# Router logits with stationary router weights, and the counts and context sums in another order

## The reference

```python
p_group = softmax(t @ wg + bg)                     # 4 groups
p_top_g, g_idx = top_k(p_group, 1)
e_logits = einsum('td,gde->tge', t, we) + be        # 4 x 8 experts
e_logits = take_along_axis(e_logits, g_idx[:, :, None], axis=1)[:, 0]
p_top_e, e_idx = top_k(softmax(e_logits), 2)
w_sel = p_top_g * p_top_e / sum(p_top_e)
# combine: w_sel at the two chosen experts of the chosen group, else 0
hid = silu(t @ w_gate[e]) * (t @ w_up[e]) * combine[:, e]     # 32 experts, 512 wide
out = sum over e of hid @ w_down[e]
```

## Time and profile before

| | |
|---|---|
| median of three runs | 1970.4 us (1968.82 to 1971.67) |
| profiled execution | 1971.46 us, its span 1969.6 us |
| busy in the span: TensorE, weight loads, VectorE, ScalarE, GpSimd | 1868.5, 1366.6, 818.2, 586.1, 387.5 us |
| mean granted TensorE clock | 0.978 |
| DMA | 429.84 MB, mean 218 GB/s |
| router: first transpose to first expert's rows | 405.78 to 430.09 us |
| expert stage, end of its last load wait | about 867 us |

### The profile page before, as it was taken

One profiled execution on the slowest core, in us unless ns is written; L12 is line 12 of the kernel. 1 busy time (PEld: TensorE's weight loads), 2 busy tenths in 40 slices (PEclk: granted clock), 3 DMA queues, 4 the chain that ended last, 5 costly groups with the idle time before them and its releaser, 6 DMA issues.

```text
span 1969.6 us, 26164 instructions
## 1 busy us (share of the span) xinstructions
PE 1868.5 (95%) x11248; PEld 1366.6 (69%) x11248; DVE 818.2 (42%) x1342; ACT 586.1 (30%) x892; POOL 387.5 (20%) x205
## 2 busy tenths in 40 slices
PE   5999999999999999999999899999999899889998
PEld 2777796964444343447887657888888688679998
DVE  1615255731111111116343744566655625574333
ACT  2513103331111111113113535223333411544554
POOL 2000000120000000004003132333443210425665
PEclk8999999989999999999999899999999899999999
DMA  9479917669999999992224004454445222414451
GB/s 357 153 256 344 341 44 278 215 270 429 426 427 428 427 427 427 427 394 82 86 86 161 3 33 171 150 181 162 149 150 182 92 91 89 171 47 168 174 196 38
DMA packets 111425, 429.84 MB, mean 218 GB/s; under 512 B 5706, under 2 KB 8821, under 8 KB 98512
## 3 DMA queue, kind: packets, MB, share of 16 engines
q1 hardware_dynamic: 109056, 416.56, 54.5%
q0 software_dynamic: 2256, 11.62, 1.6%
HBM read 427.11 MB, written 1.05 MB: 217 GB/s over the span
## 4 chain that ended last, share of the span: by engine, by line
PE 65%; DMA 17%; DVE 5%; PEld 5%; issue 3%; ACT 3%; POOL 2%; PEldq 0%; SPq 0%; POOLq 0%; DVEq 0%; ACTq 0%
PE bank L556 64%; DMA ring<-in_moe_w_down 7%; PEld bank L556 4%; DMA H<-in_moe_w_down 4%; DMA arena<-in_moe_w_down 4%; DMA ring<-in_ada_w 2%; PE bank L571 1%; PEldq L535 0%; POOL arena L1889 0%; POOL arena L1888 0%; DVE H L1976 0%; DMA ring<-in_w_in 0%; DVE H_low L1983 0%; POOL arena L1893 0%; POOL arena L1891 0%
## 5 line engine op out<-in xcount | busy, mean ns | idle before, releaser
L556 PE MATMUL bank<-arena_r 128*128 128x256 f32 (+1 forms) x2176 | 591.7, 339 | 12.1 <-ACT arena_r L1380 6.1
L556 PE MATMUL bank<-arena_r,ring_low 128*128 128x512 f32 (+2 forms) x1920 | 596.4, 342 | 1.8 <-DVE H_low L1983 1.0
L556 PEld LDWEIGHTS bank<-arena_r 128*128 128x128 f32 x2176 | 384.9, 190 | 63.2 <-issue 18.2
L556 PE MATMUL bank<-arena 128*128 128x64 bf16 (+8 forms) x2908 | 366.1, 319 | 42.7 <-DMA arena<-in_hy_filt_w 11.7
L556 PEld LDWEIGHTS bank<-arena_r,ring_low 128*128 128x128 f32 (+1 forms) x1920 | 352.5, 188 | 47.7 <-issue 2.7
L556 PEld LDWEIGHTS bank<-arena 128*128 128x128 bf16 (+4 forms) x2908 | 206.2, 132 | 203.8 <-issue 168.6
L556 PE MATMUL bank<-H_low,arena_r 128*128 128x512 f32 (+1 forms) x672 | 217.3, 340 | 0.0
L556 PE MATMUL bank<-ring,arena 128*64 128x512 f32 x768 | 172.0, 603 | 8.4 <-DMA ring<-in_moe_w_down 7.9
L2556 DVE SCALAR_TENSOR_TENSOR X<-bank,mod,X 128x256 f32<-128x256 f32 x216 | 94.2, 478 | 196.6 <-PE bank L556 196.6
L1915 POOL TENSOR_TENSOR ring_low<-ring,arena_r 128x2048 fp32r<-128x2048 f32 x31 | 142.3, 4614 | 131.1 <-DVE ring_low L2568 69.1
L1394 ACT ACTIVATE arena<-bank 128x512 f32<-128x512 f32 (+2 forms) x106 | 51.2, 496 | 368.5 <-PE bank L556 368.5
(11 more groups left out here) (304 smaller groups left out, 1845.4 us busy)
## 6 DMA issues: line engine op xcount, KB each, us to landing
ring<-in_w_mlp SPq DMA_DIRECT2D x32, 2048.0 KB, 7.8
ring<-in_w_in SPq DMA_DIRECT2D x26, 2048.0 KB, 9.1
ring<-in_ada_w SPq DMA_DIRECT2D x24, 2048.0 KB, 11.6
ring<-in_moe_w_up SPq DMA_DIRECT2D x17, 2048.0 KB, 23.2
ring<-in_moe_w_gate SPq DMA_DIRECT2D x17, 2048.0 KB, 27.8
arena<-in_moe_w_up SPq DMA_DIRECT2D x15, 2048.0 KB, 22.4
ring<-in_moe_w_down SPq DMA_DIRECT2D x14, 2048.0 KB, 23.3
arena<-in_moe_w_down SPq DMA_DIRECT2D x13, 2048.0 KB, 24.3
```

What stands on the lines that cost most here:

```text
L556: ins = nc.tensor.matmul(o, l, r, start=start, stop=stop, skip_group_check=True)
```

## The change

The logits are computed first: `WR[:, k]` (36 columns) is stationary and the 256 tokens move, one product for each block of `H` as it is normed, into 36 partitions of bank 4. ACT copies them to `LGT`, and two products with the identity turn them back to 2 x 36 columns for VectorE. The transposes of the first token block stand between, those of the second behind. VectorE does two of its four subtractions ahead of the router's logic and two behind it; ACT's exponentials stand between its two middle parts. Only one of the count steps stays ahead of the one-hot columns, the rest goes behind the pair's weights. The first four context sums move from behind the zero products to behind the ranks, the other four behind the first two gathers, and the context's root on ACT behind two copies. Chunk 7 waits for "tokens_passed" 6.

```diff
@@ SP, expert()
                 elif c == MRING - 1:
-                    sp.wait_ge(S("logits"), 1)
+                    sp.wait_ge(S("tokens_passed"), 6)
@@ tiles
+        LGT = A(5000, L)
@@ TensorE
+            def tokens(tb):
+
+                for k in range(KT):
+                    tr(ps[2 * tb + k // 4][:, (k % 4) * P:(k % 4 + 1) * P], H[:, k, tb * P:(tb + 1) * P], "tokens_passed" if k % 4 == 3 else None)
+
+            pe.wait_ge(S("tables_in"), 64)
+            for k in range(KT):
+                pe.wait_ge(S("normed"), 16 + k + 1)
+                mm(ps[4][0:NR, 0:L], WR[:, k, :], H[:, k, 0:L], k == 0, k == KT - 1, "logits" if k == KT - 1 else None)
+            tokens(0)
+            pe.wait_ge(S("rt_exp"), 1)
             for tb in range(TB):
-                for k in range(KT):
-                    if tb == 0:
-                        pe.wait_ge(S("normed"), 16 + k + 1)
-                    tr(ps[2 * tb + k // 4][:, (k % 4) * P:(k % 4 + 1) * P], H[:, k, tb * P:(tb + 1) * P], "tokens_passed" if k % 4 == 3 else None)
-            pe.wait_ge(S("tables_in"), 64)
-            for tb in range(TB):
-                for k in range(KT):
-                    mm(ps[4][:, tb * NR:(tb + 1) * NR], H[:, k, tb * P:(tb + 1) * P], WR[:, k, :], k == 0, k == KT - 1,
-                       "logits" if (tb, k) == (1, 7) else None)
+                mm(ps[4][:, L + tb * NR:L + (tb + 1) * NR], LGT[0:NR, tb * P:(tb + 1) * P], ident[0:NR, 0:NR], inc="logits" if tb else None)
+            tokens(1)
 
             pe.wait_ge(S("selected"), 1)
             pe.wait_ge(S("h_rest"), 4)
             for b in range(4):
                 mm(ps[b], SW[:, 0, :], SW[:, 0:4, :], True, False)
-            for k in range(KT // 2):
-                stat(2, k, L, CSQ)
...
-            for k in range(KT // 2, KT):
+            for k in range(KT // 2):
                 stat(2, k, L, CSQ)
...
             for u in range(2):
                 gather(u, 4 + u, "gathered")
+            for k in range(KT // 2, KT):
+                stat(2, k, L, CSQ)
@@ ScalarE
+            act.wait_ge(S("logits"), 1)
+            A_(LGT[0:NR, :], ps[4][0:NR, 0:L], ACT.Copy).then_inc(S("rt_exp"), 1)
             for b in range(4):
                 act.wait_ge(S("tokens_passed"), 2 + b + 1)
                 A_(by_blocks(HB[:, 0, b // 2, :], b % 2), ps[b][:, :].rearrange("t (p k) -> t k p", k=KT), ACT.Copy).then_inc(S("h_natural"), 1)
...
+            middle_part(0)
+            router_exp(0)
+            router_exp(1)
+            middle_part(1)
             act.wait_ge(S("b2_in"), 16)
             for k in range(KT):
                 square(k, L, CSQ, X[:, :, L:2 * L]).then_inc(S("squares"), 1)
...
+            gathered_out(0)
+            gathered_out(1)
             act.wait_ge(S("sum_ready"), 3)
             link(A_(RS[:, L:2 * L], ps[6][:, 0:L], ACT.Ln, bias=vec("eps")))
             A_(RS[:, L:2 * L], RS[:, L:2 * L], ACT.Exp, scale=-0.5).then_inc(S("rms_ready"), 1)
-            gathered_out(0)
-            gathered_out(1)
@@ VectorE
+            rest_of(0)
+            rest_of(1)
+            dve.wait_ge(S("logits"), 2)
+            link(V.tensor_tensor(LG, ps[4][:, L:L + 2 * NR].rearrange("p (a b) -> p a b", a=2),
                                  bc(vec("rbias", 0, NR).unsqueeze(1), [P, TB, NR]), ALU.add))
...
             V.tensor_tensor(ex, m2, m1, ALU.subtract).then_inc(S("rt_arg"), 1)
-            dve.wait_ge(S("rt_exp"), 2)
+            rest_of(2)
+            rest_of(3)
+            dve.wait_ge(S("rt_exp"), 3)
...
             dve.wait_ge(S("ranks"), 1)
             dve.wait_ge(S("selected"), 2)
+            cnt, over = RT[0:1, 300:301], RT[0:1, 301:304]
+            V.tensor_reduce(cnt, ps[5][0:1, 2 * NX:3 * NX], AX.X, ALU.max)
...
             onehots(0)
             pair_weights(0)
+            for k in range(3):
+                i = V.tensor_scalar(over[:, k:k + 1], cnt, float(CAP * (k + 1)), None, ALU.is_gt)
+            link(i)
+            link(V.tensor_reduce(RT[0:1, 304:305], over, AX.X, ALU.add))
+            V.tensor_copy(npass[0:1, 0:1], RT[0:1, 304:305]).then_inc(S("passes_known"), 1)
```

More of the change, by code:

```diff
@@ L1547, in _, with middle_part, router_exp @@
                 A_(by_blocks(HB[:, 0, b // 2, :], b % 2), ps[b][:, :].rearrange("t (p k) -> t k p", k=KT), ACT.Copy).then_inc(S("h_natural"), 1)
-            for tb in range(TB):
+            def middle_part(tb):
                 act.wait_ge(S("h_rest"), 2 * tb + 2)
                 A_(HB[:, 1, tb, :], HN[:, tb, :], ACT.Copy).then_inc(S("h_natural"), 1)
+            def router_exp(i):
+                act.wait_ge(S("rt_arg"), i + 1)
+                o = RT[:, 16:24] if i == 0 else RT[:, 200:202]
+                A_(o, o, ACT.Exp).then_inc(S("rt_exp"), 1)
+            middle_part(0)
+            router_exp(0)
+            router_exp(1)
+            middle_part(1)
             act.wait_ge(S("b2_in"), 16)
@@ L1553, in _ @@
                 square(k, L, CSQ, X[:, :, L:2 * L]).then_inc(S("squares"), 1)
[L1554 to L1557, removed]
             def gathered_out(e):
@@ L2217, in _, with rest_of @@
             V.memset(CMB[:, :, NX:NX + 4], 0.0)
-            for b in range(4):
+            def rest_of(b):
                 dve.wait_ge(S("h_natural"), b + 1)
@@ L2221, in _ @@
                                 by_blocks(HB[:, 0, b // 2, :], b % 2), ALU.subtract).then_inc(S("h_rest"), 1)
-            dve.wait_ge(S("logits"), 1)
-            link(V.tensor_tensor(LG, ps[4][:, 0:2 * NR].rearrange("p (a b) -> p a b", a=2),
+            rest_of(0)
+            rest_of(1)
+            dve.wait_ge(S("logits"), 2)
+            link(V.tensor_tensor(LG, ps[4][:, L:L + 2 * NR].rearrange("p (a b) -> p a b", a=2),
                                  bc(vec("rbias", 0, NR).unsqueeze(1), [P, TB, NR]), ALU.add))
```

## The result

| | before | changed |
|---|---|---|
| median, both run side by side | 1971.59 us (1968.82 to 1978.54) | 1977.23 us (1971.29 to 1989.05) |
| profiled execution, span | 1971.46 us, 1969.6 us | 1971.29 us, 1969.4 us |
| ratio | | 1.0031, interval 1.0018 to 1.0043 |
| first TensorE work of the router to `rows(0)` | 24.31 us | 29.35 us |
| issue of the ninth load | 438.06 us | 442.63 us |

The changed kernel is slower by 0.3%, some 6 us. The range held it; the side of the 0.2% that I had favoured (no change that can be measured, 0.59) was not the one that came (slower, 0.37), though the interval's lower end, 1.0018, lies just under that line. The profiled execution of the changed kernel is by chance its fastest one and no longer than that of the kernel before, so the two spans must not be subtracted. What can be compared is the router stage, counted from its first TensorE instruction.

The account below looks back on a forecast made before the run. The end of the load stream follows the release behind `rows(0)`, so only that start counts. Ranks +2.7, to the gather -0.6 and sums +1.75 give +3.8 us on 1970.4: 1974.2 us, range 1968.5 to 1977.8.

Parts of the forecast that it names:

- the 0.2%: Whole time: 3.9 us, about what measurement can tell from no change; within 0.59, slower 0.37, faster 0.04.
- What bounds it: Expert stage: a saturated load stream with one gap of 10 to 11 us, ended by the release following `rows(0)`.
- rival D: Load stream: the gap hides every shift because its end is not tied to this release; 1970.4 us, chance 0.05.
- Part 1: Router start: logits first as wide products let VectorE start 3.8 us early, bounds 1.9 to 5.5.
- Part 2: Fourth subtraction: done 5.5 us after router start, plus 2.0 us for GpSimd colliding with VectorE, at 421.1 us.
- rivals A and B: Router: A, no collision, 1972.2 us, chance 0.22; B, clock stays high and no collision, 1968.6 us, chance 0.13.
- Part 3: Zero products behind idle TensorE: start at half clock, take 5.3 us (3.5 to 7.0), ranks 2.7 us late.
- Part 4: Ranks to gather: count chain but its first step moves behind the one-hot columns, 2.85 us, 0.6 gained.
- Part 5: Four context sums behind the gathers: nothing covers them, `rows(0)` moves 1.75 us later, bounds 1.7 to 1.9.
- Part 6: Free edits: eighth load some 4 us earlier into a full stream, context's root and ACT's squares; no effect.
- Rival C: Router: low clock through logits and zero products, and full collisions; 1977.9 us, chance 0.10.

Follow-up runs that it names:

- pool_late: Changed kernel with GpSimd's two subtractions waiting for the finished selection; 1976.07 us, ratio 1.0014.
- short_path3: Changed kernel, subtractions ahead of the router, GpSimd's second block late, one count chain, five context sums ahead of the ranks, other reorderings; 1972.37 us, ratio 1.0005.
- before_again: The kernel before, without any edit, measured against itself; 1972.48 us, ratio 0.9990.
- count_once: Changed kernel with the early copy of the count chain removed; 1973.88 us in a single execution.
- rests_pool: Changed kernel with all four VectorE subtractions ahead of the router and GpSimd's behind the selection; 1981.45 us in a single execution.
- zeros_split: Changed kernel with two zero products ahead of the router and two left behind it; 1977.07 us in a single execution.

## Why the prediction was right or wrong

**What bounds it: right.** The ninth load moved with `rows(0)` (7.97 us behind it in both kernels), the last load moved by 4.8 us, and rival D, the gap as cover, is out: over 14 traces the ninth load lies anywhere from 30.6 to 38.8 us behind the start of the stage, and the last one 400.2 to 402.2 us behind it each time.

**Part 1, early logits: right.** Predicted bias 3.8 us early, at 7.8 us behind the first product; measured 7.75, 3.86 early. The wide products brought the clock back while they ran, as assumed. Bounds were not needed.

**Part 2, fourth subtraction and collision: right in mechanism and size.** 5.5 us with 2.0 for the collision gave the zero products at 421.1 - 405.78 = 15.3; they began at 14.98. The stretched operation cost 1.98 - 0.17 = 1.8 us, and pool_late takes exactly that away; rivals A and B are out. The Trainium skill, "SBUF — State Buffer", section "Who interferes with whom", has it that an operation of VectorE with two SBUF inputs contends with a GpSimd instruction that reads SBUF. The trace agrees, 1.98 us beside 2.12, and operations of 0.17 us are not too small for it. By the same section of the Trainium skill `tensor_scalar` can contend too, in its two-port modes; the 1.43 us of short_path3 agree with that.

**Part 3, zero products: right in mechanism, sized too low.** Taken 5.3 us to the ranks, measured 426.43 - 420.29 = 6.1, within the bounds of 3.5 and 7.0. The step that failed is "some 3.6 us at half": the granted clock was 0.50 in all of 420 to 424 and 0.78 in 424 to 428, which puts its return near 425.8 and makes it 5.5 us at half. I had scaled the time at half clock from the 2.6 us of the kernel before, where narrow products had been running ahead; here 7.08 us of idle TensorE were. pool_late (5.27 us idle, 5.3 us for the products) and before_again (no idle time, but 6.40 us) show that it isn't the idle time alone. The Trainium skill, "TensorE: Matmul & The Clock Gate", section "HAM oscillation — how this bites in real kernels", describes work that starts at the lower clock behind a gap; the trace agrees on the start, 0.50. With the start 0.34 early, the ranks were 0.5 us later than forecast.

**Part 4, ranks to gather: wrong, a misreading of the diff.** I wrote that all but one step of the count chain moves behind the one-hot columns, and the description of the change says so too. It does not: the diff adds a reduction (L2300) ahead of VectorE's rank operations and a second chain behind the pair's weights, and leaves the first where it was (L2304 to L2310 of the changed kernel). What the title and the text ahead of the prediction say of the counts holds for the second copy only. Instead of -0.6 the term was +0.1: 3.53 us from the ranks to the gathers, before 3.45; from the second rank product 3.30 and 3.21. count_once, which does what I had described, gives the 0.6 (2.71 against 3.30). Of the three terms of the sum it has the largest error. (The zero products alone were sized 0.8 us too low, but 0.3 of that was met by their earlier start.)

**Part 5, sums: right.** Predicted 1.75, bounds 1.7 to 1.9; gathers to `rows(0)` grew from 2.89 to 4.70, by 1.8.

**Part 6: right.** The eighth load went out at 413.24, 4.1 us early, into a full stream, for nothing.

**The sum.** Forecast +2.7 - 0.6 + 1.75 = +3.8; measured on the path +3.14 + 0.09 + 1.81 = +5.0 (against before_again's trace +3.8, by the low clock of its zero products; that the forecast is met there is chance). Of the 1.2 us between them 0.7 is the misread part and the rest the zero products. The time says +6.1 (3.5 to 8.5), or 5.9 over three comparisons. The 1 us above the path is within the interval and its cause is not shown; the three comparisons of the changed kernel differ by far more among themselves (2.4 to 9.1 us), so that the time lies so near the path's 5.0 is in part luck; the wait behind the branch is a candidate. Rival C had the low clock of the zero products right and that of the logits wrong. Had I read part 4 rightly, the forecast would have been 4.4 us late, beyond the 3.9 of the 0.2%.

## What to carry to other kernels

In a kernel whose end is tied to a saturated stream of loads, find the one gap in the stream and price a change only by what it does to the release that ends it; of 3.85 us won at the start of that path 1.4 arrived. A wait that is moved behind a chain takes all with it that stands behind it on its engine: here cheap fill-in work lost its cover and paid the low clock as well, and taking it off the path handed the low clock to the next work in line. Lay the long GpSimd operation beside the chain of short VectorE operations that will now run with it, and check in the new file, not in the diff, that what is said to move is gone from its old place.

## What the runs showed of the hardware

- A VectorE `tensor_tensor` on 128 x 32, 128 x 16 or even 128 x 8 elements takes 1.98 to 2.11 us instead of 0.17 when it meets a GpSimd subtraction of 2.12 us; it is one operation of the chain that pays, the ones behind it are short again. So the price of a meeting is what is left of GpSimd's operation, however little VectorE does.
- Not every operation in the midst of a subtraction pays. One that reads one of its two inputs from a bank keeps its 0.20 us (L2305 of short_path3 at 422.48), and a small `tensor_reduce` its 0.14 (L2310 of rests_pool at 431.17); a `tensor_scalar` of 128 x 64 pays (L2306 of short_path3, 1.43 us instead of 0.20).
- In zeros_split the low clock was moved by filling a part of the idle stretch, not got rid of: 1.96 us of work at full clock were put into it, and the clock was 0.50 in 424 to 428 all the same. short_path3, whose longest idle stretches of TensorE between 412 and 428 were 1.67 and 1.39 us, kept 1.00 throughout.
- Two executions of one and the same kernel differ in the router by up to 1.25 us (before and before_again) and over the whole by 10 us (1969.4 and 1979.9). The places found are those of low clock and the wait behind a branch, which has two lengths, 1.63 us (8 traces) and 4.5 to 4.9 (6 traces); why is not shown.
